# One gated product earlier: reordering ScalarE and VectorE work between the recurrence and the fifth attention head

## The reference

```
mod = c @ ada_w + ada_b                       # six vectors of 1024: sh1, sc1, gt1, sh2, sc2, gt2
h = rmsnorm(x, norm1_g) * (1 + sc1) + sh1
xr, yr, q, k, v, ga, gb = split(h @ w_in)     # each 256 x 1024
xr = causal_dwconv(xr)
y_a = rg_lru(xr, ...) * gelu(yr)              # gated linear recurrence over time
q, k = head_rmsnorm(q), head_rmsnorm(k)       # 8 heads of 128
y_b = stick_breaking_attention(q, k, v)
mix = sigmoid(ga) * y_a + sigmoid(gb) * y_b
x = x + gt1 * (mix @ w_out)
```

## Time and profile before

| | us |
|---|---|
| median of 3 runs | 1652.8 |
| lowest, highest run | 1652.63, 1653.83 |
| the profiled execution's own time | 1653.83 |
| its span (first to last instruction) | 1652.0 |
| PE busy in the span | 1579.9 |
| DVE busy | 651.1 |
| ACT busy | 339.8 |

### The profile page before, as it was taken

How to read it: one execution, slowest core, us unless ns; L and a number is a source line. 1 busy time by engine, 2 the same in 40 slices (tenths; PEclk the granted TensorE clock), 3 DMA queues, 4 the chain that set the end, 5 groups by cost and what they waited for, 6 DMA issues and landing times. The chain is left out here.

```text
span 1652.0 us, 20624 instructions
## 1 busy us (share of the span) xinstructions
PE 1579.9 (96%) x7276; PEld 892.9 (54%) x7276; DVE 651.1 (39%) x1450; ACT 339.8 (21%) x657; POOL 0.8 (0%) x5
## 2 busy tenths in 40 slices
PE   5999999999999999899999988999999899999997
PEld 4888888888888885333333332333333333333332
DVE  6667862889810662332222222122222312222223
ACT  3126662433300253210001000000010001000001
POOL 0000000000000000000000000000000000000000
PEclk9999999999999999799999999999999899999999
DMA  9936683549953421389999999999999999999995
GB/s 396 419 131 252 255 353 123 195 176 364 417 227 121 153 103 52 142 354 421 420 420 420 420 420 420 409 409 420 420 420 420 420 397 383 421 420 420 420 420 222
DMA packets 77108, 544.94 MB, mean 330 GB/s; under 512 B 8960, under 2 KB 9472, under 8 KB 11424
## 3 DMA queue, kind: packets, MB, share of 16 engines
q1 hardware_dynamic: 75904, 541.79, 81.0%
q10 hardware_dynamic: 1024, 1.18, 0.2%
q0 software_dynamic: 32, 0.00, 0.0%
HBM read 541.89 MB, written 1.05 MB: 329 GB/s over the span
## 5 line engine op out<-in xcount | busy, mean ns | idle before, releaser
L1110 PE MATMUL bank<-ring,scr 128*64 128x512 f32 x2048 | 453.6, 599 | 3.8 <-DMA ring<-in_w_mlp 3.8
L541 PE MATMUL bank<-hT,ring 128*128 128x256 f32 x1472 | 321.6, 379 | 0.0
L1110 PEld LDWEIGHTS bank<-ring,scr 128*64 128x64 f32 x2048 | 163.3, 139 | 276.8 <-issue 260.3
L541 PEld LDWEIGHTS bank<-hT,ring 128*128 128x128 f32 x1472 | 279.0, 190 | 40.0 <-issue 2.7
L1143 PE MATMUL bank<-ring,hT 128*64 128x512 f32 x1024 | 233.8, 597 | 1.4 <-DMA ring<-in_w_mlp 1.4
L2534 DVE TENSOR_SCALAR scr<-bank 128x256 f32<-128x256 f32 x64 | 27.0, 422 | 361.6 <-PE bank L1110 361.6
L1143 PEld LDWEIGHTS bank<-ring,hT 128*64 128x64 f32 x1024 | 72.5, 136 | 135.7 <-issue 130.2
L1673 ACT ACTIVATE scr<-scr 128x256 f32<-128x256 f32 x64 | 26.7, 418 | 508.9 <-DVE scr L2534 508.9
L2425 DVE TENSOR_TENSOR scr<-bank,mc 128x512 f32<-128x512 f32 x34 | 23.5, 692 | 261.1 <-PE bank L1042 231.5
L1796 DVE SCALAR_TENSOR_TENSOR ring<-ring,cb 128x1024 f32<-128x1024 f32 x80 | 94.6, 1220 | 0.0
L742 PE MATMUL bank<-scr,ring 128*128 128x256 f32 x384 | 83.5, 379 | 1.6 <-ACT scr L1494 1.6
(11 more groups left out here) (420 smaller groups left out, 1469.7 us busy)
## 6 DMA issues: line engine op xcount, KB each, us to landing
ring<-in_w_mlp SPq DMA_DIRECT2D x384, 1024.0 KB, 20.0
ring<-in_w_in SPq DMA_DIRECT2D x28, 1024.0 KB, 15.6
ring<-in_up SPq DMA_DIRECT2D x24, 1024.0 KB, 7.1
ring<-in_w_ada SPq DMA_DIRECT2D x24, 1024.0 KB, 6.8
ring<-in_ada_w SPq DMA_DIRECT2D x16, 1024.0 KB, 5.4
ring<-in_down SPq DMA_DIRECT2D x12, 1024.0 KB, 15.5
ring<-in_ada SPq DMA_DIRECT2D x8, 1024.0 KB, 19.9
ring<-in_w2in SPq DMA_DIRECT2D x6, 1024.0 KB, 12.8
```

The lines of the kernel that those rows point to most:

```text
L541: ins = mm(b[:, 256 * j:256 * j + 256], v[:, k * 256 + j * 128:k * 256 + j * 128 + 128], rhs[:, k, :], start=(k == 0), stop=(k == 7))
L1110: ins = mm(HID[0][n][64 * hf:64 * hf + 64, :], K.xe[0][x % 2][:, xo:xo + 64], v[:, o0:o0 + 512], start=False, stop=(k == 7), skip_group_ch ...
```

## The change

On ScalarE, `att_step(8)` (the Abs, Exp and Ln of head 4) moves from ahead of the four sigmoids of `ga` to between the first and the second of them. On VectorE, `att_step(8)` (the copy of head 3's output and `att_first` of head 4) moves likewise from ahead of the four products to behind the first of them. The `ada(2, 0)` that stood ahead of it moves behind the first product too, so that the pieces `ada(2, 0)` and `ada(2, 1)` come between the first product and `att_step(8)`. The `table(ACT.Exp)` ahead of `att_step(12)` goes. TensorE's and SyncE's lists keep their order.

```diff
@@ scalar_program
         if c == 3:
             att_step(7)
         gates_last(c)
-    att_step(8)
     for c in range(4):
-        if c >= 2:
+        if c:
             att_step(7 + c)
         landed(("ga", c))
         if c < 2:
@@
         act(K.Wt[2 + c % 2], K.main_bank(("ga", c))[:, :], ACT.Sigmoid).then_inc(S.ga, 1)
     for c in range(4):
-        if c == 1:
-            table(ACT.Exp)
         att_step((11, 12, 13, 15)[c])
         if c == 2:
             att_step(14)
@@ vector_program
         recurrence_last(c)
-    ada(2, 0)
-    att_step(8)
     for c in range(4):
-        if c >= 2:
+        if c:
             att_step(7 + c)
         mix = K.pair(K.mix, c)
         e.wait_ge(S.ga, c + 1)
         e.wait_ge(S.mixr, c + 1)
         tt_(mix, mix, K.Wt[2 + c % 2], ALU.mult).then_inc(S.mixga, 1)
+        if c == 0:
+            ada(2, 0)
         ada(2, c + 1)
```

## The result

The changed kernel takes 1662.51 us as the median of five runs (1660.65 to 1662.82), the kernel before 1652.8 (five runs, 1652.2 to 1654.66). The ratio is 1.0052 with a 95% interval from 1.0039 to 1.0064: 8.6 us slower, between 6.4 and 10.6. The ratio comes from the single runs and is not that of the two medians, which lie 9.7 us apart. All 25 executions of the changed kernel on record have a median of 1661.34 (1657.85 to 1666.37), 8.5 us over the 1652.8. The forecast was 1662.0, the range 1657.3 to 1665.5.

The account below looks back on a forecast made before the run. TensorE, busy 96% of the span, was taken as the bound. Terms 4.85 + 1.28 + 2.3 + 0.8 = 9.2 us gave 1662.0 against the 1652.8 median; the 8-in-10 range was 1657.3 to 1665.5.

Parts of the forecast that it names:

- Exp load at head 6: Between Abs and Exp on ScalarE: a load there adds 1.28 us, so TensorE's 0.66 us wait becomes 1.94.
- clock behind the first stall: TensorE behind head 4's 4.75 us stall: the granted clock falls, costing 2.3 us, between 1.5 and 3.3.
- clock behind head 6's wait: TensorE behind the 1.94 us wait at head 6: a possible clock fall, taken as 0.8 us, between 0 and 1.8.
- The first stall: TensorE at head 4's sums: start at 212.15 in place of 207.40, 4.75 us, 4.85 with the slower first pair.
- The case of the free load: Rival at ScalarE's first sigmoid: its table load does not stand behind the wait; 8.0 us, time 1660.8; chance 0.10.
- the case built on the drain: Rival: each table switch on the path also costs a drain, 2.8 us more; 12.0 us, time 1664.8; chance 0.02.
- The 1.83 us behind a wait of 1.52: TensorE's eight matmuls of L1031 took 3.55 us instead of 1.72; read as 1.83 us lost to the clock.
- the stretch at 0.50 from 689 to within 695: Clock low while TensorE worked throughout: about 6.6 us at half clock, read as 3.3 us lost, the clock term's upper end.
- Carried to the end: From the stage to the kernel's end: the expert weights' stream shifts with TensorE, so the delay carries through at full size.
- the case "given back": Rival at the expert stage's start: queued weights let TensorE win the delay back, so not slower; chance 0.05.
- The idle DMA stretch at 715: DMA engines nearly idle (0.20) from 715 to 720 us: the weight stream starts when TensorE frees ring slots.
- Nothing is late a second time: Behind head 4's sums: its logits, the second sigmoid's load and SyncE's later transfers cost nothing more.

Follow-up runs that it names:

- e10: The changed kernel measured again with no edits; 1662.64 us, 1.0051 over the kernel before.
- e1: The changed kernel with the early load of the exponential's table put back ahead of head 6; 1660.1 us, 1.0038 over the kernel before.
- e7: The kernel before with two more ada pieces on VectorE ahead of head 4's copy and att_first; 1660.61 us, 1.0043.
- e2: The changed kernel with head 4's copy and att_first directly behind the first product, both ada pieces behind them; 1661.0 us, 1.0048 over the kernel before.
- e3: The changed kernel with a one-element Sigmoid ahead of the wait for the recurrence, loading the table early; 1660.51 us, 1.0044 over the kernel before.
- e4: The kernel before with only the early load of the exponential's table taken out; 1654.9 us beside 1653.71, 1.0008.
- e9: The kernel before, TensorE only: the two halves of gb's second projection issued apart with step 12 between; 1651.69 us beside 1653.68, 0.9993.
- e5: The changed kernel with early Exp load back, both ada pieces behind head 4's att_first, and first sigmoid's table load early; 1657.67 us, 1.0026 over before.
- e6: The kernel before with one more ada piece on VectorE ahead of head 4's copy and att_first; 1656.61 us, 1.0020.
- e11: The kernel before, profiled once more with no edits; one execution, 1655.65 us, span 1653.8.
- e8: The kernel before with head 4's copy and att_first ahead of both ada pieces on VectorE; 1654.34 us beside 1652.58, 1.0013.

## Why the prediction was right

The table sets its terms beside what the profiles have; the clock's rows use all profiled executions with such a stall.

| term | forecast, us | measured, us |
|---|---|---|
| end of head 4's `att_first` | 212.10 | 211.93 |
| later start of head 4's sums | 4.75 | 4.83 |
| slower first pair | 0.10 | 0.10 |
| Exp load at head 6 | 1.28 | 1.28 (0.66 to 1.94) |
| clock behind the first stall | 2.3 (1.5 to 3.3) | 1.42, 1.69, 3.03 (changed, e10, e1), 2.82 (e7) |
| clock behind head 6's wait | 0.8 (0 to 1.8) | 0, 0, 1.46, 0, 1.46 (changed, e10, e2, e3, e4) |
| total | 9.2 | 8.6 [6.4, 10.6] |

**The first stall** was right by its own steps. The recurrence's end released a table load and not a sigmoid; e3, which takes the load off that wait, shortens the stall by the load's 1.3 us. VectorE's list, not ScalarE's chain, came last, by 1.4 us as forecast; e2 removes VectorE's 4.6 us and finds the chain behind it. The case of the free load (0.10) is excluded by the row at 203.47. The drain that the Trainium skill adds to every load ("ScalarE: Activation LUTs", "What ACT_TABLE_LOAD costs") does not show here either, on neither side of a load. The load at 205.76 starts 0.02 behind the end of Abs, and the sigmoid starts 1.30 behind the start of its load, as before; the case built on the drain (0.02) is out.

**The Exp load** was right: the same 1.94 us in every profile without the early load, 0.66 in every one with it but e9's, whose TensorE list has no wait there at all.

**The clock** was right in its mean, 2.24 and 0.58 us measured for 2.3 and 0.8, and in part by luck, since its readings were weaker than they looked. The 1.83 us behind a wait of 1.52 were no loss to the kernel (above). And the stretch at 0.50 from 689 to within 695 is 6.3 us by its slices, not 6.6, and only the end of a longer one: the granted clock of the kernel before had been at its lower level since 674.9, through several waits. So the 3.3 was no upper bound taken from a single fall; the longest loss measured in this stage, 3.03 in e1, happens to lie under it.

That a stall over 4 us brings a fall held in four of four profiles. Behind 3.39 us (e3) and 3.29 (e2) it did not fall; behind about 2 us it fell once (e5, 1.7 us lost) and once not (e6); behind head 6's 1.94 it fell in two of five. The rows of before suggested that stalls of 1.5 us and more bring it as a rule; below 4 us it is a matter of chance. The timed runs give the mean without profiles: their mean spans over before's are 7.35 us for e3, whose profile has 4.9 us of stage growth and no fall, and 7.2 for e7 with 4.5 us of stage growth beside its clock. So by this estimate about 2.5 us come on average with such stalls, if nothing else is in it; with five and six runs it is uncertain by some 1 us.

**Carried to the end** was right, with an argument weaker than it read. In the stages up to 451 us nothing is given back. TensorE's first row of the first block's down projection, before and now:

```profile
451.34 41.71 PE L742 MATMUL bank<-scr,ring 128*128 128x256 f32 x192 [1.60 <-ACT scr L1494]
```

```profile
458.73 41.71 PE L742 MATMUL bank<-scr,ring 128*128 128x256 f32 x192 [1.60 <-ACT scr L1491]
```

Counted from head 4's scores it comes 258.70 us later in place of 251.07. That is 7.63 more, just what the stage grew by, and in every other profile too the two agree to 0.01 us: 2.25 and 2.26 in e6, 2.65 and 2.65 in e4, 7.34 and 7.35 in e7, and the 1.24 that e9 gained. Behind that the profiles say nothing on the change. The expert stage's first row of the changed kernel:

```profile
696.12 0.26 PE L1206 MATMUL bank<-scr 32*1 32x32 f32 x2 [1.26 <-issue]
```

It is 7.04 us later than in the first profile of before and 3.66 later than in e11, the same kernel. From the start of L742 to this row the thirteen profiles have 236.6 to 241.3 us, the two of before 237.7 and 241.3; from this row to the end they have 959.2 to 964.2, before 962.9 and 961.3, the changed kernel 960.1. So its span, only 4.2 us longer than in the first profile, gave nothing back that executions of one kernel do not differ by anyway. Had only this execution been at hand, the case "given back" would have looked half right. The runs exclude it: the growth of the stage in the profiles of e6, e7 and the changed kernel (2.25, 7.34 and 7.63 us) lies inside the intervals of what they cost in time (3.3, 7.1 and 8.6). The idle DMA stretch at 715 that I argued from moved with TensorE (the changed kernel has a DMA share of 1.01 there and of 0.08 from 722 to 727), which fits the argument, but e6 and e7 are the proof.

**Nothing is late a second time** was right for the changed kernel, where head 4's weights are done at 215.84 and used at 221.28. It did not follow that the place has slack: e2 and e8 made the same weights late by moving ada pieces behind `att_first`.

What stays open: how the chance of a fall depends on the stall's length below 4 us (the profiles are too few), what e5 costs beyond its stage, and whether e9's gain is real in the time.

## What to carry to other kernels

- In strictly ordered lists, moving an instruction that waits ahead of work that is ready costs the wait, and everything that came along with it: here a wait for the recurrence, a table load that stood behind it, and 2.3 us of unrelated work. Before moving work, read for the engine that bounds the kernel how early each of its inputs is now (0.2 us was all the slack), and how early each of its results is wanted on the other side of the place.
- A table load made early while the engine idles is worth its full length where the chain behind it has no slack, and the busy shares of the two engines show nothing of that.
- A stall on TensorE of several microseconds costs more than itself, by half or so here by the best estimates. A single profiled execution can be some microseconds off in total while its waits in a stage repeat to 0.01 us; what the clock takes behind them does not repeat (1.42 and 1.69). Sum the stage from the profile and judge the total from many runs.
- Time that matmuls lose to the clock counts only where the next instruction on TensorE starts later for it. Read the start of what follows, not the duration.

## What the runs showed of the hardware

- A semaphore wait can sit on the table load rather than on the activation behind it. It then delays both (start at 203.47, released by VectorE), and a one-element activation ahead of it takes the load out (e3, 1.3 us).
- Without any edit, executions of the kernel before differ by more than its first three runs suggested: the runs beside e5 to e8 spread from 1650.24 to 1658.1, and the two profiles of it have the same stage. The clock goes with it: those two executions have a mean granted clock of 0.986 and 0.980. The same 1.52 us wait in the expert stage was followed by half clock in one execution and not in the other (3.55 and 1.94 us for the same eight matmuls), and what waits behind them started 3.71 us behind the first of the eight in both.
- The fall of the granted clock came before TensorE went on or only after it: about 1.1 us before in e7 (0.79 in the slice from 210, sums at 211.67), about 1.2 us after in e5 (0.51 in the slice from 211, sums at 209.78).
